# Two waits for the first gathers taken out of the expert stages' weight prologue

## The chip, the cores and the metric

The kernel runs on one core of one Trainium2 chip. Its time is device microseconds; the median of three runs is 1151.69 us (1151.37 to 1151.73). One execution was also recorded by the hardware profiler, and all rows below come from that one.

## The reference

A two-layer encoder step for 512 prompt tokens and 64 sample tokens of width 1024. Layer 0 mixes with pooling and sparse attention, layer 1 with a gated spatial unit. After each mixer stands a mixture of experts, which is what the change touches:

```python
def hier_moe(h, w_rg, w_re, w_gate, w_up, w_down):
    ...   # a token chooses one group of 8 experts, then 2 experts in it
    return routed_experts(xt, expert_id, gates, w_gate, w_up, w_down).reshape(B, T, D)

def expert_block(args):
    xb, e = args
    return (jax.nn.silu(xb @ w_gate[e]) * (xb @ w_up[e])) @ w_down[e]
```

There are 32 experts with three weight matrices of 1 MB each, so a layer reads 96 MB of expert weights. The 576 tokens make 1152 assignments to experts.

## The kernel before, in words

An expert stage (one for each layer) walks over 16 pairs of experts, 64 token slots for each expert, so that a pair fills the 128 partitions. For a pair, GpSimd gathers 128 token rows out of `h_rows` in DRAM into `xg` by an indirect DMA (`gather`, L564; a slot without a token moves nothing). TensorE turns them (`turn_rows`, L1591, recorded at L1300), ScalarE copies the result into `xT`, TensorE multiplies by gate and up weights (`up`, L1599), and after SiLU and product by the down weights (`down`, L1612). The result is scattered to `y_rows` (`scatter`, L571). For pair `i` the gather of pair `i + 2` is issued once the rows of pair `i + 1` are turned in the main loop; the gathers of pairs 0 and 1 go out at the start, back to back (L595 and L596), as soon as the slot table `tab` is written and the normed rows are in DRAM.

The indirect DMAs of GpSimd run on one DMA queue (q0 in the profile), all weights are issued by the sync engine (SP) on another (q1). Both share the core's 16 DMA engines.

The weights have two buffers of six blocks in `ring` (`wgu[0]`, `wdn[0]`, `wgu[1]`, `wdn[1]`) and a third in memory that the dense layers have left (`wgu[2]` in `dw`, `wdn[2]` in `hT`). A prologue fills all three, 18 blocks of 1 MB for pairs 0 to 2, each block as soon as its memory is free. `gate_ups` and `downs` issue the blocks, `third_pair` those of `wgu[2]`. After the prologue `sp` issues `load_gain` (the norm's gain for the next layer, broadcast to all partitions) and enters `experts(l)` (L374). There `gu(3, 0, 1)` waits until TensorE has finished the first pair's gate and up products (`s_gud`), and issues pair 3's blocks; each later pair's blocks wait in the same manner for the pair that used the buffer. All of it is one instruction stream on SP, in the order of the code.

In the prologue of layer 0 the two blocks of `third_pair(0, 0)` (L474), in that of layer 1 the second half of `gate_ups(1, 2, ...)` (L505) and both `downs(1, 4, ...)` (L506), stand behind waits for `s_xg`, the semaphores that the first two gathers raise when they have landed (L472, L473 and L503, L504; in the trace the first has the line of a helper, L416).

Slots beyond an expert's 64 are worked off after the 16 pairs, as extra pairs, whose weights are loaded then. TensorE's first instruction of the stage, `turned(0, 0, 1, True)` (L1641), waits for the first gather alone.

Of the kernel before, what the change touches and what calls it, by code (L numbers as in the profile page):

```python
# [95 lines left out]
def build(nc, a, out):  # L96

    es = ExitStack()
    with es:
# [182 lines left out]
        s_xg = [[sem(f"gathered{l}{b}") for b in range(2)] for l in L2]  # L282
# [45 lines left out]
        def _(sp):  # L328
# [29 lines left out]
            def gate_ups(l, e0, dst, signal, ks=(0, 1)):  # L358
                for k in ks:
                    for i, w in enumerate(("moe_w_gate", "moe_w_up")):  # L360
                        sp.dma_start(dst[:, k, i], a[w][l, bass.ds(e0 + k, 1)]  # L361
                                     .rearrange("e (p c) n -> p (e c) n", c=C)).then_inc(signal, 16)
# [52 lines left out]
            def third_pair(l, k):  # L415
                sp.wait_ge(s_dwf, 6 * (l + 1) + 1 - k)  # L416
                gate_ups(l, 4, wgu[2], s_wgu[l][2], (k,))
# [51 lines left out]
            store_rows(1, 0, range(4, NT))  # L469
            gate_ups(0, 2, wgu[1], s_wgu[0][1], (1,))  # L470
            third_pair(0, 1)
            for b in range(2):  # L472
                sp.wait_ge(s_xg[0][b], 16)  # L473
            third_pair(0, 0)  # L474
            load_gain(2)
            experts(0)
# [23 lines left out]
            store_rows(3, 1, range(3, NT))  # L500
            gate_ups(1, 2, wgu[1], s_wgu[1][1], (0,))
            third_pair(1, 0)
            for b in range(2):  # L503
                sp.wait_ge(s_xg[1][b], 16)  # L504
            gate_ups(1, 2, wgu[1], s_wgu[1][1], (1,))  # L505
            downs(1, 4, wdn[2], s_wd[1][2])  # L506
            load_gain(4)
# [790 lines left out]
        def _(pe):  # L1298
# [68 lines left out]
            for task in tasks:  # L1367
                if task[0] == "proj":
                    _, q, j = task
                    for _ in proj_steps(q, j):  # L1370
                        pass
# [97 lines left out]
            def probs_turn(g):  # L1469
                b = g // NKV  # L1470
                r = ROWS[b]
                pe.wait_ge(s_te, min(max(7, 6 + g), 11))
                if g:
                    pe.wait_ge(s_pte, 2 * g)
                if g >= 8 and g % 4 == 3:
                    pe.wait_ge(s_ht, NT + g // 4 - 1)
                for u in (2 * g, 2 * g + 1):
                    pe.wait_ge(s_pr, u + 1)
                    for c, (k, _) in enumerate(chunks(b)):
                        ins = turn(ps[u % 2][0:k, c * P:c * P + r], sm[0:r, u % 4, c * P:c * P + k], r)  # L1480
                    ins.then_inc(s_ptp, 1)
# [277 lines left out]
```

## Time and profile before

| what | us |
|---|---|
| median of three runs | 1151.69 |
| the profiled execution, whole | 1152.18 |
| its span, first to last instruction | 1150.3 |
| TensorE busy | 926.5 (81%) |
| mean granted TensorE clock | 0.919 of full speed |
| DMA traffic of the weights' queue (q1) | 259.16 MB |
| DMA traffic of GpSimd's queue (q0) | 18.90 MB |
| expert stage of layer 0, first gather to last scatter in the chain of waits | 336.3 to 593.2 |
| expert stage of layer 1, the same | 846.1 to 1118.9 |

The engines run side by side, so their busy times don't add up to the span. What sets the end is read from the chain of waits; what a DMA queue holds at a moment is read from the issue times on SP and from windows that give the mean busy share of the 16 DMA engines and the bytes that they move.

### The profile page before, as it was taken

The numbers are of one execution on the slowest core, as the hardware profiler recorded it, in microseconds if no ns is written. First come the engines' busy times: TensorE is split into PE (matmuls) and PEld (weight loads), VectorE is DVE, ScalarE is ACT, GpSimd is POOL, SyncE is SP. The second block draws the span as 40 slices with busy tenths as digits, with TensorE's granted clock in tenths as the row PEclk, the third lists the DMA queues.
The fourth block names the chain that finished last, engine by engine and source line by source line (L and its number), as shares of the span: only waits on it lengthen the run. The fifth ranks groups of instructions, "written<-read, shape, count | busy, mean of one in ns | idle before, by whom it ended". The sixth has DMA issues, their size and how long they took to land.

```text
span 1150.3 us, 12314 instructions
## 1 busy us (share of the span) xinstructions
PE 926.5 (81%) x4396; PEld 510.1 (44%) x4396; DVE 358.8 (31%) x903; ACT 279.5 (24%) x590; POOL 203.9 (18%) x266
## 2 busy tenths in 40 slices
PE   6999979999829987887837998999749978778750
PEld 4566545455514432332315776877524433233220
DVE  3048994443351111000129139202431110010017
ACT  4132234455311111111125322332201111011012
POOL 0000810000011211111133433550011221111110
PEclk9999999999959999988977999999859998998995
DMA  8210143300469999999973420242569999999936
GB/s 274 74 58 1 58 147 128 141 19 20 189 254 367 362 420 422 420 422 420 413 267 99 151 80 9 74 146 111 225 269 412 379 418 421 421 421 419 386 132 238
DMA packets 66679, 278.65 MB, mean 242 GB/s; under 512 B 15837, under 2 KB 22877, under 8 KB 40138
## 3 DMA queue, kind: packets, MB, share of 16 engines
q1 hardware_dynamic: 56842, 259.16, 57.1%
q0 software_dynamic: 9792, 18.90, 4.4%
q8 instruction: 28, 0.46, 0.2%
q14 instruction: 17, 0.14, 0.0%
HBM read 268.76 MB, written 26.03 MB: 256 GB/s over the span
## 4 chain that ended last, share of the span: by engine, by line
PE 56%; DMA 23%; DVE 9%; ACT 4%; POOL 4%; issue 3%; SPq 1%; POOLq 0%; ACTq 0%; DVEq 0%
DMA ring<-in_moe_w_up 20%; PE bank L1599 15%; PE bank L1323 12%; PE bank L1334 11%; PE bank L1300 5%; PE bank L1612 4%; PE bank L1382 3%; PE bank L1446 1%; PE bank L1494 1%; POOL mid L545 1%; DVE x L1237 1%; DVE mid L954 1%; SPq L361 1%; PE bank L1461 1%; ACT mid L652 1%
## 5 line engine op out<-in xcount | busy, mean ns | idle before, releaser
L1599 PE MATMUL bank<-ring,mid 128*64 128x512 f32 x992 | 242.9, 646 | 61.5 <-DMA ring<-in_moe_w_up 57.6
L1599 PEld LDWEIGHTS bank<-ring,mid 128*64 128x64 f32 x992 | 81.9, 149 | 219.3 <-issue 205.7
L652 ACT ACTIVATE mid<-bank 128x512 f32<-128x512 f32 (+6 forms) x182 | 84.7, 508 | 265.1 <-PE bank L1612 124.1
L1300 PE MATMUL bank<-con,mid 128*128 128x128 f32 (+3 forms) x654 | 102.4, 297 | 53.9 <-DVE mid L954 37.7
L1300 PEld LDWEIGHTS bank<-con,mid 128*128 128x128 f32 (+3 forms) x654 | 85.2, 186 | 101.0 <-issue 50.3
L1612 PE MATMUL bank<-ring,mid 128*64 128x512 f32 x496 | 113.3, 597 | 18.6 <-issue 12.9
L1206 DVE TENSOR_TENSOR mid<-mid,bank 128x256 f32<-128x256 f32 x32 | 13.5, 421 | 310.0 <-ACT mid L849 310.0
L1334 PE MATMUL bank<-dw,hT 128*128 128x402 f32 (+1 forms) x384 | 106.3, 461 | 0.6 <-PE bank L1334 0.6
L1323 PE MATMUL bank<-dw_high,hT_high 128*128 128x512 f32 (+1 forms) x240 | 95.9, 399 | 2.6 <-POOL dw_low L582 1.7
L1323 PE MATMUL bank<-dw_low,hT_high 128*128 128x512 f32 (+1 forms) x240 | 94.1, 392 | 0.0
L1323 PE MATMUL bank<-dw_high,hT_low 128*128 128x512 f32 (+1 forms) x240 | 93.9, 391 | 0.0
L849 ACT ACTIVATE mid<-bank 128x256 f32<-128x256 f32 x32 | 12.3, 385 | 285.0 <-PE bank L1599 285.0
L1334 PEld LDWEIGHTS bank<-dw,hT 128*128 128x128 f32 (+1 forms) x384 | 57.8, 177 | 42.0 <-issue 8.4
L561 POOL COPY six<-tab 128x2 int32 (+1 forms) x32 | 5.7, 178 | 372.2 <-DVE mid L1214 372.2
L1612 PEld LDWEIGHTS bank<-ring,mid 128*64 128x64 f32 x496 | 38.9, 136 | 71.6 <-issue 71.6
L1334 PE MATMUL bank<-dw,ring 128*128 128x512 f32 (+1 forms) x192 | 69.5, 533 | 0.3 <-PE bank L1334 0.3
L582 POOL TENSOR_TENSOR dw_low<-dw,dw_high 128x2048 fp32r<-128x2048 f32 x12 | 55.6, 4657 | 70.8 <-ACT dw_high L652 68.4
L1214 DVE COPY mid<-bank 128x512 f32<-128x512 f32 x32 | 22.1, 691 | 122.8 <-PE bank L1612 122.8
L652 ACT ACTIVATE ring<-bank 128x512 f32<-128x512 f32 (+5 forms) x86 | 35.6, 442 | 101.9 <-PE bank L1334 63.4
L561 POOL COPY gix<-tab 128x2 int32 (+1 forms) x34 | 7.5, 219 | 266.0 <-DVE tab L1182 259.1
L1323 PEld LDWEIGHTS bank<-dw_high,hT_high 128*128 128x128 f32 (+1 forms) x240 | 42.7, 178 | 15.7 <-issue 2.4
L1323 PEld LDWEIGHTS bank<-dw_high,hT_low 128*128 128x128 f32 (+1 forms) x240 | 42.8, 178 | 12.3
(181 smaller groups left out, 951.7 us busy)
## 6 DMA issues: line engine op xcount, KB each, us to landing
ring<-in_moe_w_gate SPq DMA_DIRECT2D x62, 1024.0 KB, 13.1
ring<-in_moe_w_up SPq DMA_DIRECT2D x62, 1024.0 KB, 16.5
ring<-in_moe_w_down SPq DMA_DIRECT2D x62, 1024.0 KB, 18.4
dw<-in_gm_w_in SPq DMA_DIRECT2D x4, 2048.0 KB, 20.0
ring<-y_rows SPq DMA_DIRECT2D x8, 1024.0 KB, 8.0
dw<-in_par_w_in SPq DMA_DIRECT2D x4, 1608.0 KB, 9.1
dw<-in_par_w_out SPq DMA_DIRECT2D x2, 2048.0 KB, 8.4
hT<-in_moe_w_down SPq DMA_DIRECT2D x4, 1024.0 KB, 11.2
```

The costliest lines, as they stand in the source:

```text
L561: pool.tensor_copy(dst, tab[:, bass.ds(i, 1), :].rearrange("p a v -> p (a v)")).then_inc(s_cry[l], 1)
L582: pool.tensor_tensor(dwl[:, q % 2, 4 * k:4 * k + 4, :], part, high[q - 7][:, 4 * k:4 * k + 4, :].bitcast(F32), ALU.subtract).then_inc(s_lo, 1)
L652: return act.activation(dst, src, ACT.Copy, scale=scale)
L849: act.activation(sg, ps[2 + b][:, 0:FE], ACT.Silu).then_inc(s_sg, 1)
L1206: dve.tensor_tensor(hh, sg, ps[2 + b][:, FE:2 * FE], ALU.mult).then_inc(s_hh, 1)
L1214: dve.tensor_copy(yb[:, b, 0:512], ps[6][:, :]).then_inc(s_yed, 1)
L1300: return pe.transpose(dst, src, ident[0:k, 0:k])
L1323: ins = pe.matmul(acc, left[:, c, cols], right[:, c, :], start=(n == 0), stop=(n == len(steps) - 1))
L1334: ins = pe.matmul(acc, left(c), cols, start=(c == 0), stop=(c == C - 1))
L1382: ins = pe.matmul(unit_bank(n)[:, 0:HALF], dw[:, 0, c, g * P:(g + 1) * P], hT[:, c, (m % 2) * HALF:(m % 2 + 1) * HALF], start=(c == 0), st ...
L1599: ins = pe.matmul(ps[2 + b][64 * k:64 * k + 64, :].rearrange("p (w n) -> p w n", w=2), xT[:, b, c, 64 * k:64 * k + 64], w[:, k, :, c, :], ...
L1612: ins = pe.matmul(ps[6 + hf][64 * k:64 * k + 64, :], hhT[:, b, c, 64 * k:64 * k + 64], w[:, k, c, hf * 512:hf * 512 + 512], start=(c == 0) ...
```

## The change

Both pairs of waits are taken out. `third_pair(0, 0)`, the second half of `gate_ups(1, 2, ...)` and `downs(1, 4, ...)` are then issued right behind what stands ahead of them, and so are the two `load_gain` that follow. `third_pair` still waits for `s_dwf`, and nothing else is changed.

```diff
@@ -469,8 +469,6 @@
             store_rows(1, 0, range(4, NT))
             gate_ups(0, 2, wgu[1], s_wgu[0][1], (1,))
             third_pair(0, 1)
-            for b in range(2):
-                sp.wait_ge(s_xg[0][b], 16)
             third_pair(0, 0)
             load_gain(2)
             experts(0)
@@ -500,8 +498,6 @@
             store_rows(3, 1, range(3, NT))
             gate_ups(1, 2, wgu[1], s_wgu[1][1], (0,))
             third_pair(1, 0)
-            for b in range(2):
-                sp.wait_ge(s_xg[1][b], 16)
             gate_ups(1, 2, wgu[1], s_wgu[1][1], (1,))
             downs(1, 4, wdn[2], s_wd[1][2])
             load_gain(4)
```

## Rows read from the trace of the kernel before

**Rows 1.** Page, parts 2 and 4: DMA share by slice; chain by line.

```profile
DMA  8210143300469999999973420242569999999936
...
DMA ring<-in_moe_w_up 20%; PE bank L1599 15%; PE bank L1323 12%; PE bank L1334 11%; PE bank L1300 5%; PE bank L1612 4%; PE bank L1382 3%; PE bank L1446 1%; PE bank L1494 1%; POOL mid L545 1%; DVE x L1237 1%; DVE mid L954 1%; SPq L361 1%; PE bank L1461 1%; ACT mid L652 1%
```

**Rows 2.** Waits of SP, sync's queue: total us, times, longest us.

```profile
SPq L416 <- DMA mid<-h_rows,gix: 25.1, 1, 25.1
...
SPq L504 <- DMA mid<-h_rows,gix: 22.3, 1, 22.3
```

**Rows 3.** Timeline of SP, first expert stage: start us, us, the DMA issued.

```profile
317.26 0.43 SPq L361 DMA_DIRECT2D dw<-in_moe_w_up  x1
342.86 0.33 SPq L361 DMA_DIRECT2D dw<-in_moe_w_gate  x1
...
343.71 0.43 SPq L350 DMA_DIRECT2D gain<-in_norm_mix  x1
```

**Rows 4.** Windows, first expert stage: length, engines' busy us (instructions), clock, DMA share, GB/s.

```profile
319.00:331.50 12.50, 1.33 (x21) 1.05 (x20) 10.11 (x48) 0.32 (x2) 0.00 (x0) 0.50 1.00 417
331.50:332.00 0.50, 0.00 (x0) 0.00 (x0) 0.47 (x2) 0.00 (x0) 0.00 (x0) 0.50 0.09 33
332.00:338.00 6.00, 1.16 (x20) 0.95 (x20) 4.40 (x17) 0.00 (x0) 2.43 (x5) 0.50 0.00 0
338.00:342.50 4.50, 1.64 (x8) 1.57 (x8) 0.15 (x1) 0.00 (x0) 1.10 (x2) 0.50 0.55 148
387.00:394.00 7.00, 6.44 (x34) 3.05 (x32) 0.85 (x2) 1.47 (x3) 1.88 (x4) 1.00 0.61 194
```

**Rows 5.** Chain of waits, first expert stage: start us, us, what.

```profile
336.30 4.52 DMA mid<-h_rows,gix
...
344.15 9.34 PE bank L1599 x32
```

**Rows 6.** Timeline of SP, second expert stage.

```profile
828.05 1.27 SPq L361 DMA_DIRECT2D dw<-in_moe_w_up  x1
851.67 0.33 SPq L361 DMA_DIRECT2D ring<-in_moe_w_gate  x1
...
853.68 0.44 SPq L350 DMA_DIRECT2D gain<-in_norm_final  x1
862.51 0.33 SPq L361 DMA_DIRECT2D ring<-in_moe_w_gate  x1
```

**Rows 7.** Windows, second expert stage.

```profile
830.00:841.50 11.50, 1.30 (x20) 1.05 (x20) 9.32 (x44) 0.32 (x2) 0.00 (x0) 0.50 1.02 427
842.50:847.50 5.00, 1.16 (x20) 0.95 (x20) 3.44 (x14) 0.00 (x0) 2.16 (x5) 0.50 0.00 0
847.50:851.50 4.00, 1.24 (x6) 1.24 (x7) 0.35 (x2) 0.00 (x0) 1.18 (x2) 0.50 0.42 115
854.00:864.00 10.00, 9.99 (x42) 3.87 (x38) 0.42 (x1) 1.49 (x3) 0.42 (x1) 0.83 1.01 419
898.00:904.00 6.00, 5.44 (x30) 2.72 (x28) 0.85 (x2) 1.47 (x3) 0.63 (x1) 1.00 0.74 240
```

**Rows 8.** Chain of waits, second expert stage.

```profile
846.08 4.14 DMA mid<-h_rows,gix
...
893.54 6.87 PE bank L1599 x32
...
927.60 21.93 DMA ring<-in_moe_w_up
```

**Rows 9.** DMA issues 343.9 to 344.5, third gather, first stage: us to landing last.

```profile
mid<-h_rows,gix POOLq DMA_INDIRECT x1, 9.2
```

**Rows 10.** DMA issues 853 to 854, third gather, second stage.

```profile
mid<-h_rows,gix POOLq DMA_INDIRECT x1, 8.7
```

**Rows 11.** DMA issues 388 to 390, a gather beside thinning traffic.

```profile
mid<-h_rows,gix POOLq DMA_INDIRECT x1, 4.7
```

**Rows 12.** Line 568, all 34 gathers of the main loop.

```profile
DMA to landing us min/median/max: 3.4/9.6/11.1
```

## The prediction

> **What bounds the kernel now.** First the page: the DMA engines stand at nine tenths in two long blocks of slices, and the chain of waits gives a fifth of the span to the landing of expert weights in the ring [rows 1]. These are the two expert stages. A reader could think that any weight issued earlier is time won. The stages have to be read from their start to see why not.
>
> The waits of SP come next: SP stands still for 25.1 us at the wait of layer 0 and 22.3 us at that of layer 1 [rows 2]. That is what the change takes out, but it is idle time of a queue, and the question is who waits for what SP issues behind it.
>
> Layer 0: the last block ahead of the wait is issued at 317.26, the first behind it at 342.86, the gain at 343.71 [rows 3]. The DMA engines run full until 331.5 at 417 GB/s, are empty until 338.0, and then carry the gathers [rows 4]. The chain goes through the first gather (336.30, 4.52 us) to the first pair's gate and up products, which start at 344.15 [rows 5]. The held blocks are not in it: they are pair 2's.
>
> Layer 1 has the same shape. Last block ahead at 828.05, first behind at 851.67, gain at 853.68, pair 3's first block at 862.51 [rows 6]. DMA is full at 427 GB/s until 841.5, empty from 842.5 to 847.5, and carries only the gathers until 851.5, at 115 GB/s [rows 7]. The chain: gather at 846.08 for 4.14 us, then TensorE's work pair after pair; only from 927.60 on does it go over the landing of weights, for 21.93 us at a time [rows 8].
>
> What decides is the point where the weight stream takes over. Between 898 and 904 DMA is at 0.74 of its share, moving 240 GB/s [rows 7], and between 387 and 394 of layer 0 at 0.61, moving 194 GB/s [rows 4]: the queue has run dry, because pair 5's blocks wait until TensorE has finished with pair 3's buffer (its up products run from 893.54 for 6.87 us [rows 8]). Up to there TensorE sets the pace, not the weights; from there on the stream runs full and sets the end. So the start of the lasting stream hangs on TensorE, TensorE hangs on the first gather, and each us that the first gather is late comes out at the end in full.
>
> **The change part by part.** *The waits removed.* Two waits on SP in each layer; they cost SP idle time that hides nothing and is in no chain. Worth 0. The later waits of SP (pair 3's blocks wait for the first pair's up products) keep their times, and that is what is late next on SP.
>
> *Moved in layer 0.* Two blocks of 1,024 KB and the gain of 512 KB, 2.10 + 0.52 = 2.62 MB, now queued right behind 317.26. At 0.417 MB per us that is 6.3 us; the queue that ran dry at 331.5 now runs dry at 337.8. The first gather's bytes start at 338.0 [rows 4]. They just miss each other. A gather beside thinning traffic took 4.7 us [rows 11] against 4.52 alone [rows 5]: I take +0.2 us. Below 0 it cannot go, since nothing of the gather is made shorter; above, if the tail were late and the gather stood fully in traffic, 9.2 - 4.52 = +4.7 us [rows 5, 9]. Nothing is won by the earlier landing: the blocks are for pair 2, whose products come two pairs later, and TensorE waits for no weights there.
>
> *Moved in layer 1.* Four blocks of 1,024 KB and the gain, 4.19 + 0.52 = 4.71 MB, are now issued from about 829.3 on (the last issue ahead begins at 828.05 and takes 1.27 us [rows 6]). At 0.42 MB per us they take 11.2 us from about 841.8, to 853.0; the two gathers in the same time move 4.0 us x 115 GB/s = 0.46 MB, another 1.1 us, so the queues run dry at about 854. The first gather is issued at 846.08 and its bytes moved from 847.5 on [rows 7, 8]: now in the middle of that traffic. No row shows a first gather in traffic, so I go by third gathers, which are issued when the two ahead of them have landed and no scatter stands before them on their queue. The one of layer 0 is issued just when the held blocks go out, and took 9.2 us [rows 9]; that of layer 1 took 8.7 [rows 10]. Against 4.14 [rows 8] that is +5.1 and +4.6 us. Bounds: nothing of the gather's own way gets shorter, so no gain; as little as 4.7 - 4.14 = +0.6 us by the gather in thinning traffic [rows 11], as much as 11.1 - 4.14 = +7.0 by the slowest of the 34 [rows 12]. I take the mean of the two near rows, +4.8 us: the median of all, 9.6, includes many that stand behind a scatter. It also fits the end of the traffic: the gather would land at 846.1 + 8.95 = 855.0, one us after the queue has run dry.
>
> The second gather, queued behind the first, is first needed after pair 0's up products, which take 9 us, so it is covered up to a landing near 867. Pair 1's and pair 2's weights, now landed by 854, were early enough before.
>
> *After it.* The granted clock stands at 0.50, the level of 1.2 GHz, while TensorE waits for the gather, and is 0.83 on average over 854 to 864, the first up products [rows 7]; a longer wait starts and ends at the same level, so I put no price on it. Pairs 0 to 4 take as long as before. SP's blocks of pair 3 go out 4.8 us later, at 867.3, now into an empty queue (before, the moved blocks still filled it from 854 to 864 at 419 GB/s [rows 7]). Two pairs of 6.3 MB at 0.42 MB per us take 30 us, about 33 with the gathers and scatters, and end near 902; pair 5's blocks come at 900.4 + 4.8 = 905.2, so the queue still runs dry first and nothing of the delay is caught up.
>
> *Sum.* 0 for the waits, +0.2 in layer 0, +4.8 in layer 1: +5.0 us. The profiled execution took 1152.18 (span 1150.3), so 1157.2 on its scale; the median of the runs is 0.49 lower, which gives **1156.7 us**.
>
> **Rivals.**
>
> *A. The DMA engines give the gather its turn.* If the two queues took turns evenly, the gather's 0.23 MB (half of 0.46) would be met by as much weight traffic at 0.42 MB per us, +0.5 us; or, if the 2 us in which its bytes move were doubled, +2.0. Time: 1152.2 to 1153.7, no difference that can be measured. The Trainium skill, page "DMA: Bandwidth & Descriptors", section "Queues, rings and completion order", says that each DMA engine goes round the queues that have work, one packet at a time; by even turns of that kind the sum would be this rival's. No run here shows how long a packet is, and the trace speaks against the even split: weight traffic costs a gather 4.6 to 5.1 us [rows 8 to 10], many times its share of bytes. Chance 0.12.
>
> *B. Layer 0 is hit too.* The margin between 337.8 and 338.0 is thin. If the first gather of layer 0 stands in traffic like the third, +4.7 instead of +0.2: 1161.2. Against it: the engines were at 1.00 to the end and stopped within half a us [rows 4], so there is little to be late. Chance 0.05.
>
> *C. Faster.* In layer 1 the moved blocks are out of the way when pair 3's are issued at 862.51; before they held the queue for some 1.5 us longer, to 864. If the stream and not TensorE decided when pair 5's blocks can go, and the gather were not slowed by more than that, the end would come 1.5 us earlier: 1150.2. It decides only if no gap stood at 898 to 904; the gap is there [rows 7]. Chance 0.03.
>
> That in layer 0 the change does almost nothing (the queue is merely emptied later, before anyone needs it) is part of the forecast itself.
>
> **How the numbers follow.** The forecast has 0.80, A 0.12, B 0.05, C 0.03. A measurement of this kernel tells about 0.2% from no change, 2.3 us, so the line lies at 1154.0. Slower: forecast and B, 0.85. Same: A, 0.12. Faster: C, 0.03. The range goes from the top of A, 1153.7 (the gather's moving time merely doubled), to 1152.18 - 0.49 + 0.2 + 7.0, rounded up to 1159.0 (the slowest gather of the trace). It leaves out A, B and C, 0.20.
>
> **What would show it.** SP's two waits for gathers are gone, and the moved blocks issued at about 317.7 and 829.3. Layer 0: DMA full to about 337.8, the first gather's landing near 4.7 us, the first up products near 344.3. Layer 1: DMA without a gap from 830 to about 854, the first gather landing about 9 us after its issue, the first up products near 858.5 instead of 853.55, pair 3's blocks near 867.5, and a gap in the DMA near 903 to 909, as wide as before. The forecast is wrong if the gather in layer 1 lands within 6 us of its issue, or if it is late and the gap near 903 has closed, so that the end is later by less than the gather.

## The result, and the profile after

Eight runs of the changed kernel have a median of 1156.24 us, eight of the kernel before 1151.53; the ratio is 1.0049 with a 95% interval of 1.0037 to 1.0061, so the changed kernel is 4.3 to 7.0 us slower (the two medians are 4.7 us apart). The forecast was 1156.7. The profiled execution's span is 1154.7 us against 1150.3. Line numbers are 2 to 4 lower behind the removed lines (L1595 after is L1599 before).

Layer 0 first. On SP the two waits for gathers are gone, and the held blocks and the gain follow at once (timeline: start us, us, the DMA issued), as against [rows 3]:

```profile
315.73 0.43 SPq L361 DMA_DIRECT2D dw<-in_moe_w_gate  x1
316.21 0.45 SPq L361 DMA_DIRECT2D dw<-in_moe_w_up  x1
316.70 0.62 SPq L350 DMA_DIRECT2D gain<-in_norm_mix  x1
```

The DMA engines then, in the same columns as [rows 4] (length, busy us and instructions of TensorE, of its weight loads, of VectorE, ScalarE and GpSimd, then the granted clock, DMA share, GB/s), and the first gather in the chain of waits (start us, us, what), against [rows 5]:

```profile
331.50:335.50 4.00, 0.92 (x19) 0.71 (x16) 2.80 (x10) 0.00 (x0) 2.04 (x3) 0.50 0.99 411
336.00:340.50 4.50, 1.73 (x8) 1.57 (x8) 0.14 (x1) 0.00 (x0) 1.08 (x2) 0.50 0.54 149
```

```profile
334.29 4.44 DMA mid<-h_rows,gix
```

This execution reaches layer 0's expert stage 2.0 us earlier than the one of before, so 335.5 here is 337.5 there. The queue is full until 335.5, six us longer than before on the same scale, and what follows from 336.0 at 149 GB/s is the gathers, alone. The first one took 4.44 us (4.52 before). They just missed each other, as forecast.

Layer 1. SP, against [rows 6]:

```profile
828.34 0.74 SPq L361 DMA_DIRECT2D ring<-in_moe_w_gate  x1
829.13 0.51 SPq L361 DMA_DIRECT2D ring<-in_moe_w_up  x1
...
830.72 0.43 SPq L350 DMA_DIRECT2D gain<-in_norm_final  x1
866.05 0.33 SPq L361 DMA_DIRECT2D ring<-in_moe_w_gate  x1
```

The windows, against [rows 7]:

```profile
842.50:847.50 5.00, 1.07 (x20) 0.86 (x20) 3.22 (x13) 0.00 (x0) 2.35 (x6) 0.50 1.01 423
847.50:853.00 5.50, 0.00 (x0) 0.00 (x0) 0.00 (x0) 0.00 (x0) 0.99 (x1) 0.50 0.99 402
854.00:857.50 3.50, 2.17 (x10) 1.21 (x10) 0.00 (x0) 2.28 (x3) 1.39 (x3) 0.50 0.00 0
900.00:907.00 7.00, 6.44 (x36) 3.13 (x34) 0.85 (x2) 1.47 (x3) 1.56 (x4) 1.00 0.56 182
```

And the chain of waits, against [rows 8]:

```profile
845.36 7.74 DMA mid<-h_rows,gix
...
856.44 9.59 PE bank L1595 x32
...
897.08 6.87 PE bank L1595 x32
...
931.10 21.69 DMA ring<-in_moe_w_up
...
1087.99 9.89 PE bank L1595 x32
...
1120.63 2.65 DMA y_rows<-mid,six
```

Where the DMA engines stood empty from 842.5 to 847.5 they now move 423 GB/s, and from 847.5 to 853.0, with the gathers among it, 402; by 854 they are empty. The first gather, issued at 845.36 in the middle of this, took 7.74 us instead of 4.14. The first up products took 9.59 us instead of 8.93. From the gather's issue to the end of those products it is 20.66 us (866.02 - 845.36) where it was 16.40: 4.26 us late. The DMA has its gap after pair 3 as before (182 GB/s from 900 to 907), and the first long wait for weights starts 85.74 us after the gather's issue instead of 81.52: still 4.22 us late. Nothing of it was caught up. The last pair (pair 15; one extra pair follows it) and the last scatter of the kernel before were these:

```profile
1084.64 8.81 PE bank L1599 x32
...
1116.21 2.65 DMA y_rows<-mid,six
```

The last pair's up products start 242.63 us after the first gather's issue, where it was 238.56, so they are 4.07 us late. They then took 9.89 us instead of 8.81, and in this execution the last scatter comes 275.27 us after the gather's issue instead of 270.13, 5.1 us late.

### The profile page after: what moved, and what is told of

The parts are those of the page before. It is cut to its first block, busy times and chain, and to the rows that moved or that the text cites. A ratio compares the mean times of both kernels' runs of the same rounds, so it can differ in the third digit from the quotient of the medians.

```text
span 1154.7 us, 12312 instructions
## 1 busy us (share of the span) xinstructions
PE 934.6 (81%) x4396; PEld 514.3 (45%) x4396; DVE 359.3 (31%) x903; ACT 279.4 (24%) x590; POOL 203.9 (18%) x266
## 4 chain that ended last, share of the span: by engine, by line
PE 57%; DMA 23%; DVE 8%; ACT 4%; POOL 4%; issue 3%; SPq 1%; POOLq 0%; ACTq 0%; DVEq 0%
DMA ring<-in_moe_w_up 20%; PE bank L1595 16%; PE bank L1319 12%; PE bank L1330 11%; PE bank L1296 5%; PE bank L1608 4%; PE bank L1378 3%; PE bank L1442 2%; PE bank L1490 1%; POOL mid L541 1%; DVE x L1233 1%; SPq L361 1%; DMA mid<-h_rows,gix 1%; DVE mid L950 1%; PE bank L1457 1%
## 5 line engine op out<-in xcount | busy, mean ns | idle before, releaser
L1595 PE MATMUL bank<-ring,mid 128*64 128x512 f32 x992 | 250.3, 662 | 55.5 <-DMA ring<-in_moe_w_up 51.5
L1595 PEld LDWEIGHTS bank<-ring,mid 128*64 128x64 f32 x992 | 84.7, 152 | 217.8 <-issue 205.9
L1608 PE MATMUL bank<-ring,mid 128*64 128x512 f32 x496 | 113.3, 597 | 18.6 <-issue 13.0
L1608 PEld LDWEIGHTS bank<-ring,mid 128*64 128x64 f32 x496 | 39.0, 136 | 71.6 <-issue 71.6
```

Of the source, the lines that this page charges most:

```text
L1595: ins = pe.matmul(ps[2 + b][64 * k:64 * k + 64, :].rearrange("p (w n) -> p w n", w=2), xT[:, b, c, 64 * k:64 * k + 64], w[:, k, :, c, :], ...
L1608: ins = pe.matmul(ps[6 + hf][64 * k:64 * k + 64, :], hhT[:, b, c, 64 * k:64 * k + 64], w[:, k, c, hf * 512:hf * 512 + 512], start=(c == 0) ...
```

## The experiments

Each is told with what it changes against the kernel before, and, where the argument needs it, with its first gather's line in the chain of waits (start us, us from issue to landing). The ratios are to the kernel before, run on the same chip.

**One layer at a time.** First layer 0 alone:

```diff
             third_pair(0, 1)
-            for b in range(2):
-                sp.wait_ge(s_xg[0][b], 16)
             third_pair(0, 0)
```

> Only layer 0's wait is taken out; layer 1 keeps its own. By the prediction's theory (the queue is dry again just before the first gather's bytes move) the time is that of the kernel before, within 1 us, the first gather of layer 0 lands 4.4 to 4.8 us after its issue, and that of layer 1 takes 4.1 as before. Rival, the cost lies in issuing early at all, whatever the queue holds: half of the measured loss or more, +2 us, shows here.

Measured: 1.0002 (0.9988 to 1.0016). The first gather of each layer:

```profile
334.36 4.34 DMA mid<-h_rows,gix
...
843.60 4.08 DMA mid<-h_rows,gix
```

Then layer 1 alone:

```diff
             third_pair(1, 0)
-            for b in range(2):
-                sp.wait_ge(s_xg[1][b], 16)
             gate_ups(1, 2, wgu[1], s_wgu[1][1], (1,))
```

> Only layer 1's wait is taken out; layer 0 keeps its own. By the prediction's theory the whole loss is here: +4 to +5 us over the kernel before, the first gather of layer 1 lands 7.7 to 9 us after its issue, the first up products end 4 to 5 us later after the gather's issue than before (16.4 us there), and the gap in the DMA after pair 3 stays. Rival (the loss is spread over both layers): about +2 us.

Measured: 1.0032 (1.0020 to 1.0044), that is +3.7 us (2.3 to 5.1).

```profile
845.25 7.92 DMA mid<-h_rows,gix
```

So the loss is layer 1's, and taking layer 0's wait out costs nothing that can be measured. The ratio lies a little under the changed kernel's, with intervals that overlap; with layer 0 worth 0.0002 I take the difference for scatter. In this execution the gather took 7.92 us, as expected, but the first up products ended 3.5 us late (19.93 us after the gather's issue), under the 4 to 5 expected.

**How much is moved.** Two of layer 1's four blocks ahead of the wait:

```diff
-            for b in range(2):
-                sp.wait_ge(s_xg[1][b], 16)
             gate_ups(1, 2, wgu[1], s_wgu[1][1], (1,))
+            for b in range(2):
+                sp.wait_ge(s_xg[1][b], 16)
             downs(1, 4, wdn[2], s_wd[1][2])
```

> Layer 0 as before. In layer 1 only the two gate and up blocks are moved ahead of the wait; the two down blocks and the gain stay behind it. 2.1 MB at 0.42 MB per us are through 5.0 us after the queue went dry before, near 846.8, and the first gather's bytes began at 847.5. Theory (what counts is whether the queue still holds weights when the gather's bytes want to move): no change, within 1 us, gather 4.1 to 4.7 us. Rival (the loss goes with the bytes moved ahead): 2.1 of 4.7 MB, about +2 us, gather 5.5 to 6 us.

Measured: 0.9994 (0.9983 to 1.0006). Windows and chain:

```profile
840.50:845.80 5.30, 1.16 (x20) 0.95 (x20) 3.88 (x11) 0.00 (x0) 1.29 (x3) 0.50 1.00 419
846.80:850.80 4.00, 1.40 (x7) 1.40 (x8) 0.32 (x2) 0.00 (x0) 1.14 (x2) 0.50 0.41 115
```

```profile
845.34 4.02 DMA mid<-h_rows,gix
```

Half of the bytes cost nothing: they are through (419 GB/s to 845.8) when the gathers' bytes move (115 GB/s). The rival that counts bytes is out. With three of the four blocks ahead:

```diff
+            gate_ups(1, 2, wgu[1], s_wgu[1][1], (1,))
+            downs(1, 4, wdn[2], s_wd[1][2], (0,))
             for b in range(2):
                 sp.wait_ge(s_xg[1][b], 16)
-            gate_ups(1, 2, wgu[1], s_wgu[1][1], (1,))
-            downs(1, 4, wdn[2], s_wd[1][2])
+            downs(1, 4, wdn[2], s_wd[1][2], (1,))
```

(`downs` is given an argument that says which of its two blocks it issues)

> Layer 1 with three of its four held blocks ahead of the wait, the fourth and the gain behind it; layer 0 as before. 3.15 MB are through 7.5 us after the queue went dry before, about 3 us after the first gather's issue and 1.7 us after its bytes would begin. Whatever a gather's price is, this traffic ends before it is paid in full: it should land 1 to 2 us later than before, 5 to 6 us after its issue. If it took 8 us, a meeting with any traffic would cost the whole price.

This version ran once. The gather:

```profile
846.78 5.35 DMA mid<-h_rows,gix
```

It takes 1.2 us longer than before, as expected: the traffic ended before the whole price was due. The single run of 1156.49 us decides nothing by itself; in its trace the first up products took 10.04 us, another 1.1, and ended 2.3 us late.

**How long the queue is.** The changed kernel cannot say whether a gather costs some 8 us in weight traffic, or waits until all that was queued is through, since its queue ran dry at the moment of landing. A longer queue tells it.

```diff
             downs(1, 4, wdn[2], s_wd[1][2])
             load_gain(4)
+            sp.dma_start(spare[1], a["moe_w_down"][0, 0:4].rearrange("e r n -> (e r) n")).then_inc(s_spare, 16)
```

(and layer 1's wait out, as above)

> Layer 1's wait is taken out as in the change, layer 0 keeps its own, and behind the gain of layer 1 one more DMA of 4 MB is queued on SP that copies weights nobody uses to a spare place in DRAM, so that the queue is not dry before about 863. Theory A (a gather in weight traffic has its own price, as the later gathers show): it lands 8.7 to 11.1 us after its issue, and the time is +5 to +7 us over the kernel before. Theory B (the gather gets out only when the weights that were queued ahead of it are through; 7.7 us in the changed kernel was just that moment): it lands 15 us or more after its issue, and the time is +11 us or more. Even turns between the queues: under 6 us.

Measured: 1.0036 (1.0024 to 1.0048), +4.1 us, under the +5 to +7 of theory A. The issues of the first and of the second gather (last number: us to landing), and the chain:

```profile
mid<-h_rows,gix POOLq DMA_INDIRECT x1, 8.0
```

```profile
mid<-h_rows,gix POOLq DMA_INDIRECT x1, 18.1
```

```profile
851.58 18.14 DMA mid<-h_rows,gix
```

The first gather landed after 8.0 us, short of theory A's 8.7 to 11.1 and far from B's 15, but the second took 18.1, so long that TensorE waited for it after the first pair's products. That was in nobody's expectation, and it leaves the question open: the first gather may have got out between the weights and the copy, which stood behind it, and the second may have waited for the copy. So it was asked again with blocks of the kernel's own:

```diff
-            downs(1, 2, wdn[1], s_wd[1][1])
-            third_pair(1, 1)
             store_rows(3, 1, range(0, 3))
 ...
             downs(1, 4, wdn[2], s_wd[1][2])
+            downs(1, 2, wdn[1], s_wd[1][1])
+            third_pair(1, 1)
             load_gain(4)
```

(and layer 1's wait out)

> Asked again with weights of the same kind, since the copy between DRAM places differs from them in what it does to the engines. Layer 1's wait is out, layer 0's in; in layer 1 the four blocks of downs(1, 2) and third_pair(1, 1), which were issued long before, go to the end of the prologue, ahead of the gain. Nothing is read twice; the queue at the first gather is 4.2 MB longer and is not dry before about 863, while pair 1's down blocks are needed near 877. Theory A (a gather in weight traffic has a price of its own): it lands 8 to 9.5 us after its issue, with the weights still running for 8 us; the time is +3.5 to +6 us over the kernel before. Theory B (it gets out when all that stands queued is through): 16 to 18 us, and +10 us or more.

Measured: 1.0054 (1.0032 to 1.0075), +6.2 us, just above the +3.5 to +6 of theory A; in the profiled execution the first up products took 10.09 us, 1.2 more than before. Windows and chain:

```profile
847.00:855.00 8.00, 0.00 (x0) 0.00 (x0) 1.15 (x8) 0.00 (x0) 2.05 (x4) 0.50 1.01 415
856.00:863.00 7.00, 5.67 (x18) 2.35 (x18) 0.00 (x0) 2.37 (x3) 1.39 (x3) 0.50 1.01 418
```

```profile
846.54 8.59 DMA mid<-h_rows,gix
```

The weights run on at 418 GB/s until 863, and the gather is down at 855.1, after 8.59 us. Theory B is out. A first gather beside weights has its own price here, some 8 to 8.6 us instead of 4, and paid less where the weights ended first (5.35 us with three blocks ahead). The 18.1 us of the second gather beside the copy in DRAM are taken up in the last section.

**The same in layer 0.** If layer 0 escaped only because its queue was dry in time, more weights behind it must hit it:

```diff
             dense(6)
-            downs(0, 4, wdn[2], s_wd[0][2])
 ...
-            for b in range(2):
-                sp.wait_ge(s_xg[0][b], 16)
             third_pair(0, 0)
+            downs(0, 4, wdn[2], s_wd[0][2])
             load_gain(2)
```

> Layer 0's wait is out, layer 1's in; in layer 0 the two blocks of downs(0, 4) are issued behind third_pair(0, 0) and no longer long before, so that 2.1 MB more stand in the queue, which is then not dry before about 5 us after the first gather's bytes want to move. Nothing is read twice. Theory (the same mechanism in either layer; layer 0 escaped only by the 0.2 us that the prediction counted): the first gather of layer 0 lands 7.5 to 9.5 us after its issue, instead of 4.4, and the time is +3 to +5 us over the kernel before. Rival (layer 0 is insensitive for another reason, such as its weights being read earlier): no change.

Measured: 1.0023 (1.0005 to 1.0041), +2.6 us (0.6 to 4.7); the +3 to +5 expected lies in the upper part of this interval. Windows and chain:

```profile
337.50:343.00 5.50, 0.00 (x0) 0.00 (x0) 0.29 (x2) 0.00 (x0) 1.24 (x2) 0.50 1.01 413
```

```profile
335.97 7.98 DMA mid<-h_rows,gix
```

The gather took 7.98 us, and the layer's stage, from the first gather's issue to the last scatter in the chain, 256.89 us instead of 253.66. The mechanism is the same in either layer, and the price nearly so.

**Which gather.** Both waits kept, but each for the first gather alone:

```diff
-            for b in range(2):
-                sp.wait_ge(s_xg[1][b], 16)
+            sp.wait_ge(s_xg[1][0], 16)
```

(and likewise in layer 0)

> Both waits stay, but for the first gather alone; the second is no longer waited for, so the held blocks go out 1.4 to 2 us earlier and meet the second gather. Theory (TensorE needs the first gather at once and the second only after pair 0's up products): first gathers 4.0 to 4.5 us, time as before within 1 us. Rival (the second gather counts too): +1 us or more.

Measured: 1.0004 (0.9993 to 1.0015); first gathers 4.39 and 3.98 us. The hold need not last for the second gather. How it fares in full traffic this does not show, since it got out before the blocks' bytes came (3.3 us to landing in layer 1); TensorE wants it some 16 us after the first one's issue.

**Whether the gap ties the end to the start.** The third buffer is used again, for pair 5, so that its blocks wait for pair 2 and not for pair 3; later pairs and the extra pairs change buffers with it:

```diff
                 gu(4, 1, 2)
                 dn(4, 1, 2)
-                with sp.Fori(2, PAIRS // 2 - 1) as r:
 ...
+                gu(5, 2, 3)
+                dn(5, 2, 3)
+                gu(6, 0, 4)
 ...
```

> Both waits stay in. The third weight buffer is used a second time, for pair 5, so that its blocks are issued when pair 2's products are done and not when pair 3's are; the later pairs change buffers with it. It tells whether the gap that the DMA has before pair 5's blocks in each layer is what ties the end to TensorE's start. Theory (the stream from there on sets the end): the gaps of 2.7 us (layer 0) and 1.6 us (layer 1) close, and the time falls by 3 to 5 us. Rival (the end of a stage is set elsewhere): no change.

Measured: 0.9981 (0.9967 to 0.9996), -2.2 us, less than the 3 to 5 expected. Where the gaps were:

```profile
385.00:392.00 7.00, 6.44 (x34) 3.06 (x32) 0.84 (x2) 1.47 (x3) 1.90 (x4) 1.00 1.01 421
896.00:902.00 6.00, 5.44 (x30) 2.73 (x28) 0.85 (x2) 1.47 (x3) 0.28 (x1) 1.00 1.02 422
```

They are closed, 421 and 422 GB/s. In layer 1 the stage fell from 270.13 to 267.29 us. In layer 0 the last pair's weights were there 2.0 us earlier (237.1 us after the first gather's issue instead of 239.1), but its up products then took 8.81 us instead of 7.11, and the stage ended at 253.38 against 253.66. The windows of these products, first before, then with the third buffer:

```profile
575.30:579.00 3.70, 3.65 (x18) 1.35 (x20) 0.00 (x0) 0.00 (x0) 0.20 (x1) 1.00 0.96 346
```

```profile
571.60:576.00 4.40, 4.36 (x14) 1.33 (x16) 0.00 (x0) 0.00 (x0) 0.22 (x1) 0.61 0.96 326
```

The granted clock was 1.00 in the one and 0.61 in the other: the gain was won in the DMA and given back by TensorE.

The same with both waits taken out, the changed kernel with the gap closed:

> The changed kernel (no waits) with the third weight buffer used a second time for pair 5, as in the earlier experiment, so that the DMA does not run dry after pair 3. With the gap gone, the stream from pair 3's blocks on sets the end; those go out some 4 us later than with the waits, but into a queue that is empty, where with the waits the held blocks filled it for some 1.5 us more. Theory (in the changed kernel every us of the late gather came out at the end because the queue ran dry behind it): here 2 to 3 us of it come out, so the time is 2 to 3 us above the 1148.4 of the kernel with waits and the third buffer, near 1151. Rival (the late gather is paid in full whatever the queue does): 4 us or more above it, 1152.4 and up.

Measured: 1151.36 us, 1.0005 (0.9991 to 1.0019). The gather is as late as in the changed kernel, the DMA does not pause:

```profile
846.82 8.08 DMA mid<-h_rows,gix
```

```profile
898.00:905.00 7.00, 7.00 (x33) 2.62 (x30) 0.69 (x1) 0.70 (x2) 2.80 (x6) 1.00 1.01 418
```

The medians are 3.0 us apart (1151.36 and 1148.39), at the upper end of what was expected, but their intervals would let the rival's 4 pass. The first up products end 20.11 us after the gather's issue (16.24 with waits and third buffer), 3.9 us late. The last pair's up products show how much of this is left, first here (from the timeline of TensorE), then with waits and third buffer (from the chain of waits):

```profile
1085.14 7.09 PE L1599 MATMUL bank<-ring,mid 128*64 128x512 f32 x32 [3.78 <-DMA ring<-in_moe_w_up]
```

```profile
1079.61 8.81 PE bank L1603 x32
```

They start 238.32 and 235.72 us after the gather's issue, 2.6 us late: 1.3 of the 3.9 us were caught up. The stage is longer by only 1.3 us (268.63 against 267.29), but that is not the DMA's doing alone, since these products took 7.09 us here and 8.81 there. So the traces, one of each kernel, say that not all of the delay comes out when the queue does not run dry; the runs' times do not decide it.

**A version that beats both.** No wait in layer 0, half of the blocks ahead of the wait in layer 1, third buffer twice; the edits are those above.

> A version meant to beat both kernels: no wait in layer 0 (it cost nothing to take it out), in layer 1 only the two gate and up blocks ahead of the wait (no cost either), and the third buffer used twice. Theory: no gather is late, and in layer 1 the queue holds 2.1 MB less when pair 3's blocks are issued, so the stream starts up to 1.5 us earlier than with both waits and the third buffer: 1147 to 1148.4, about 0.3% under the kernel before. Rival: no gain over the version with waits and the third buffer, 1148.4, or the gathers late again, above 1150.

Measured: 1148.36 us, 0.9976 (0.9966 to 0.9986): 2.8 us faster than the kernel before and, by the two ratios, some 8 faster than the changed one. It is no faster than the version with both waits and the third buffer (1148.39), so the rival that saw no gain over it came true. The last pair's products of layer 1 do start 1.2 us earlier (234.5 us after the first gather's issue, 235.7 there), but take 9.79 us where they took 8.81.

## Why the prediction was right

*The place.* "0 for the waits, +0.2 in layer 0, +4.8 in layer 1": the experiments with one layer each put 0.0002 in layer 0 and 0.0032 in layer 1. Layer 0 was decided by when the queue runs dry, as said: forecast 337.8 on the scale of before, seen at 337.5. Rival B was held off by this alone, as the kernel with more weights in layer 0 shows.

*The price of the gather* was taken too high, 8.95 us where the changed kernel has 7.74 (and 7.92, 8.08 in the two kernels with the same traffic). The third gathers from which it was taken [rows 9, 10] stood in traffic that began just as they were issued; the first gather of layer 1 met the last 8 us of it and landed as it ended. The bound by the end of the traffic was the nearer guide and had been used only to support the sum: 854 was forecast and 853.5 to 854 seen, in an execution in which the gather is issued 0.7 us earlier than before. Where the weights did not end, the gather took 8.6 us.

*No price on the longer wait at the low clock* was a step without ground. In the changed kernel the first up products took 0.66 us more. These rows show why, the same engine columns, first before, then after:

```profile
853.50:857.00 3.50, 3.45 (x9) 1.12 (x11) 0.00 (x0) 1.21 (x1) 0.92 (x1) 0.50 0.99 414
857.00:862.50 5.50, 5.50 (x27) 1.88 (x23) 0.00 (x0) 0.00 (x0) 0.00 (x0) 0.97 1.01 419
```

```profile
856.00:861.50 5.50, 5.06 (x12) 1.65 (x14) 0.00 (x0) 1.58 (x2) 1.03 (x1) 0.50 0.14 39
861.50:866.00 4.50, 4.50 (x23) 1.45 (x19) 0.00 (x0) 0.00 (x0) 0.00 (x0) 1.00 0.00 0
```

Before, TensorE worked for 3.5 us at a granted 0.50 (1.2 GHz) and then at 0.97; after, for 5.1 us at 0.50 and then at 1.00 (2.4 GHz). It is not a price of the change, though: among the other late kernels it was 8.67 and 8.68 us with layer 1 alone and with the third buffer, 10.09 with more weights behind, so it goes either way and belonged in the range. In the sum, 1.2 us too much on the gather and nothing on the clock partly cancelled: 4.26 us late after the first products, 4.8 forecast. In the profiled execution the last pair's products added another 1.1 us at a clock of 0.50 (1087.9 to 1093.0), which the forecast did not have either. So the mechanism was forecast, but that the median came within 0.5 us of the number is in part luck.

One sum of the prediction does not come out: pair 3's and 4's blocks, 33 us from 867.3 on, end at 900.3 and not near 902. What was drawn from it, that the queue runs dry before 905.2, is not touched.

*"Each us that the first gather is late comes out at the end in full"* holds as far as the last pair. How late the first up products end, and how late the last pair's (pair 15's) up products of layer 1 start, both counted from the first gather's issue and against the kernel before (16.40 and 238.56 us), in the one trace of each kernel:

| kernel | first products end | last pair starts |
|---|---|---|
| two blocks ahead | -0.1 | -0.1 |
| waits for the first gather | -0.2 | -0.2 |
| three blocks ahead | +2.3 | +2.2 |
| layer 1 alone | +3.5 | +3.5 |
| copy behind the gain | +3.6 | +4.0 |
| changed kernel | +4.3 | +4.1 |
| more weights behind | +5.6 | +5.5 |

The copy's extra 0.4 holds the 0.23 us for which TensorE waited for the second gather. Where the gap in the DMA is closed, 2.6 of 3.9 us come out. That speaks for the gap as the reason, on one trace of each kernel. What the last pair's products then take adds to it or hides it, with the clock.

*The rivals.* A, even turns between the queues, gave the gather 0.5 to 2 us; weights that keep running cost it 4.45 (8.59 against 4.14), so turns that are even in bytes are out. Even in packets they nearly are. These are the two queues in the kernel with more weights behind, while the first gather's bytes moved, 850.8 to 855.1 (packets, MB, share of 16 engines' time):

```profile
q1 hardware_dynamic: 188, 1.40, 78.5%
q0 software_dynamic: 187, 0.39, 23.6%
```

The Trainium skill's rule on turns by packet (page "DMA: Bandwidth & Descriptors", section "Queues, rings and completion order") agrees with that, if the packets that the trace counts are those of the rule, which no run here shows. C, a start into an empty queue, needed the gap to be closed. There it is seen: in the version that beats both the last pair starts about 1.2 us earlier than with waits and third buffer, and its products took 1.0 us longer.

## What to carry to other kernels

Bulk loads could here run ahead of a small transfer that the critical engine waits for without cost where the queue was dry when its bytes wanted to move; where it was not, the transfer took up to twice as long (8.59 us against 4.14). To see it coming, count the bytes behind the last issue, divide by the rate of the stage, and set the time against the small transfer's issue. A wait on which the issuing engine stands for 22 us cost nothing here and kept a 4 us gather at 4 us; to hold back only what does not drain in time did as well, and not measurably better. And whether a late start comes out at the end is read from one place first: the gap in the stream that sets the end.

## What had not been expected

*The price has two parts.* Why a first gather of 0.23 MB beside weights takes some 8 us and not 5 was settled by no experiment, but the traces split the price. Before, no DMA moves from 846.1 to 847.8, and the first gather's first packet follows, 1.8 us after its issue. In the changed kernel the weights' queue is the only one that moves anything from 845.36 to 849.6:

```profile
q1 hardware_dynamic: 253, 1.81, 102.6%
```

The gather's first packet goes out 4.3 us after its issue. So 2.5 of the 3.6 us that it takes longer lie ahead of its first packet, and 1.1 behind it; where the weights ran on it was 2.5 and 2.0 us. Turns of one packet each cannot account for the first part, in which 253 packets of the weights went by. What holds back the first packet stays open.

*The copy from DRAM to DRAM.* A gather beside it took 18.1 us, where the same second gather beside weights, in the kernel with more weights behind, took 9.7 us. From 858 to 867 the two queues moved this (columns as above):

```profile
q1 hardware_dynamic: 60, 3.36, 99.7%
q0 software_dynamic: 53, 0.01, 0.6%
```

Again there are nearly as many packets of either queue, but the copy's have 56 KB on average where the weights' had 7.4 KB. That would explain the 18.1 us; no run changed the size of the packets alone, so it is argued and not shown.

*The clock at the end.* The 32 up products of a stage's last pair, which follow a wait for weights of over 20 us, took from 7.1 us (layer 0) to 10.1 (layer 1 with more weights behind), and where windows were read the long ones had the clock at 0.50 for part of them: that hid a gain of 2.0 us in one kernel and of 1.2 in another. It happens without any change too: in the kernel with layer 0 alone, whose layer 1 is as before, they took 7.09 us and the stage 268.75 us instead of 270.13.
